# Forget bias and causal mask in a two-layer attention trunk: from matmul and mask passes to one fused vector operation with a prepared bias tile

## The reference, cut to what matters

```python
def forgetting_attention(q, k, v, log_f):
    scale = d ** -0.5
    c = jnp.cumsum(log_f, axis=-1)
    ...
        sc = (jnp.einsum('bhqd,bhkd->bhqk', qb, k, ...) * scale
              + (cq[..., :, None] - c[..., None, :]))
        sc = jnp.where(kpos[None, :] <= tq[:, None], sc, -jnp.inf)
        p = jax.nn.softmax(sc, axis=-1)
        return jnp.einsum('bhqk,bhkd->bhqd', p.astype(v.dtype), v)
```

## Time and profile before

| what | value |
|---|---|
| median of 3 runs | 568.36 us (568.06 to 568.9) |
| profiled execution | 567.49 us |
| its span, first to last instruction | 565.7 us |
| granted TensorE clock, mean | 1.000 |
| PE busy | 558.7 us (99% of the span) |
| DVE busy | 342.6 us (61%) |
| POOL busy | 268.2 us (47%) |
| ACT busy | 249.7 us (44%) |
| DMA | 47.82 MB, mean 85 GB/s |

### The profile page before, as it was taken

The page is one execution under the profiler, slowest core; times in us unless marked ns, Lnnn a source line. Parts: engine busy times, 40 slices in busy tenths (PEclk is TensorE's granted clock), DMA queues, the critical chain, the costliest instruction groups (busy, mean ns, idle before and its releaser), DMA issues.

```text
span 565.7 us, 9786 instructions
## 1 busy us (share of the span) xinstructions
PE 558.7 (99%) x3118; PEld 516.2 (91%) x3118; DVE 342.6 (61%) x824; ACT 249.7 (44%) x762; POOL 268.2 (47%) x320
## 2 busy tenths in 40 slices
PE   6999999999999999999999999999999999999998
PEld 4999999999999999888888999999999999998887
DVE  3788585859594949473553755656565646464621
ACT  5737272626263636152544635444444444442400
POOL 5857272727171818162656454545353536360700
PEclk9999999999999999999999999999999999999999
DMA  9823132313131313123423261415140615030221
GB/s 263 231 61 110 57 93 57 94 56 93 56 93 56 96 52 104 45 76 110 123 68 83 83 102 34 104 35 130 28 121 24 112 30 130 24 124 2 74 94 56
DMA packets 77068, 47.82 MB, mean 85 GB/s; under 512 B 3953, under 2 KB 71281, under 8 KB 77042
## 3 DMA queue, kind: packets, MB, share of 16 engines
q1 hardware_dynamic: 77040, 47.49, 31.5%
q10 hardware_dynamic: 2, 0.00, 0.0%
HBM read 45.39 MB, written 2.10 MB: 84 GB/s over the span
## 4 chain that ended last, share of the span: by engine, by line
PE 98%; DMA 1%; SPq 0%; DVE 0%; ACT 0%; issue 0%
PE banks L325 26%; PE banks L326 26%; PE banks L327 26%; PE banks L456 5%; PE banks L441 3%; PE banks L408 2%; PE banks L426 2%; PE banks L430 2%; PE banks L425 2%; PE banks L357 1%; DMA first_raw<-in_a_w_in_dram 1%; PE banks L429 1%; PE banks L482 0%; PE banks L483 0%; SPq L292 0%; DVE hT_lo L782 0%
## 5 line engine op out<-in xcount | busy, mean ns | idle before, releaser
L1061 POOL TENSOR_TENSOR w_lo<-w_raw,w_hi 128x512 fp32r<-128x512 f32 x147 | 188.3, 1311 | 63.0 <-ACT w_hi L586 63.0
L325 PE MATMUL banks<-w_hi,hT_hi 128*128 128x384 f32 x512 | 175.6, 343 | 1.0 <-DVE hT_lo L782 1.0
L327 PE MATMUL banks<-w_hi,hT_lo 128*128 128x384 f32 x512 | 171.6, 335 | 0.0
L326 PE MATMUL banks<-w_lo,hT_hi 128*128 128x384 f32 x512 | 171.6, 335 | 0.0
L1077 POOL TENSOR_TENSOR msq<-ssq,eps 128x2 f32<-128x2 f32 x64 | 14.3, 224 | 186.4 <-ACT junk L622 186.3
L325 PEld LDWEIGHTS banks<-w_hi,hT_hi 128*128 128x128 f32 x512 | 96.5, 188 | 1.9 <-POOL w_lo L1061 1.6
L326 PEld LDWEIGHTS banks<-w_lo,hT_hi 128*128 128x128 f32 x512 | 96.5, 189 | 0.1
L327 PEld LDWEIGHTS banks<-w_hi,hT_lo 128*128 128x128 f32 x512 | 96.3, 188 | 0.0
L586 ACT ACTIVATE w_hi<-w_raw 128x512 fp32r<-128x512 f32 x148 | 85.0, 646 | 20.2 <-DMA w_raw<-in_b_w_in_dram 14.4
L622 ACT ACTIVATE junk<-banks 128x128 bf16<-128x128 f32 x128 | 34.3, 274 | 115.8 <-PE banks L327 115.8
L906 DVE RECIPROCAL gz<-gz 128x128 f32<-128x128 f32 x64 | 58.1, 931 | 0.5
(11 more groups left out here) (113 smaller groups left out, 883.9 us busy)
## 6 DMA issues: line engine op xcount, KB each, us to landing
w_raw<-in_b_w_in_dram SPq DMA_DIRECT2D x64, 256.0 KB, 3.7
w_raw<-in_a_w_in_dram SPq DMA_DIRECT2D x52, 256.0 KB, 3.0
w_raw<-in_w_out_dram SPq DMA_DIRECT2D x32, 256.0 KB, 2.9
first_raw<-in_a_w_in_dram SPq DMA_DIRECT2D x12, 256.0 KB, 5.6
out_dram<-xs SPq DMA_DIRECT2D x7, 256.0 KB, 2.1
xs<-in_x_dram SPq DMA_DIRECT2D x3, 512.0 KB, 5.8
xs<-in_x_dram SPq DMA_DIRECT2D x2, 256.0 KB, 3.2
gz<-in_norm_g_dram SPq DMA_DIRECT2D x1, 512.0 KB, 3.7
```

Source lines behind the costliest of these rows:

```text
L325: pe.matmul(dst, ah, bh, start=first and m == 0, stop=False)
L326: pe.matmul(dst, ah, bl, start=False, stop=False)
L327: mm = pe.matmul(dst, al, bh, start=False, stop=last and m == n - 1)
L1061: pool.tensor_tensor(w_lo[:, slot, k, :], raw, f32(w_hi[:, slot, k, :]), ALU.subtract).then_inc(wlo_set, by)
```

## The change

- The bias matmul L429, `pick`, `crows`, `onehot` and their preparation (`set_pick`, `split_c`, the copy L709) go. Each score tile of layer 1 has 3 matmuls, as in layer 0.
- `maxima` becomes one `tensor_tensor_reduce` for a tile: it reads the scores in PSUM and a bias tile in SBUF, writes -(score + bias) to `probs` and the minimum of it to `negmax`. Three 1-element memsets of `gate` carry the waits for the scores. In layer 0 the bias tile is a constant `strip` (zeros, and the triangular mask in its last 128 columns). `exps` then works in place on `probs`, in SBUF, with scale -1.
- In layer 1 the bias tiles stand in SBUF, all 128 partitions alike. After `cumulate` SP writes the 8 cumulated rows to DRAM (`c_rows`), waits for that, and loads the row of head 0 into four tiles with DMAs that spread it over the partitions (`load_bias`; 256, 192, 128 and 64 KB). The rows of heads 1 to 7 are loaded in the same way in the middle of a later weight job, behind its chunk 4 and behind a wait for the maxima of the head before.
- POOL adds the triangle to the diagonal blocks of the four bias tiles (`mask_bias`) as the first thing in period(h) of layer 1.

```diff
-                if layer == 1:
-                    pe.wait_ge(c_set, 1)
-                    pe.wait_ge(pick_set, h + 1)
...
-                    if layer == 1:
-
-                        pe.matmul(dst, pick[:, s, :], crows[:, 0:w], start=False, stop=False)
```

```diff
             def load_job(layer, h, src_of, bias=False):
...
                     load_chunk(w_raw[:, k % RAW, :], src_of(k), raw_in[k % RAW])
+                    if bias and k == RAW:
+                        load_bias(h - 1)
...
+            def load_bias(h):
+
+                wait(sp, max_set, TILES * (HEADS + h) if not isinstance(h, int) or h else 0)
+                for t in T_ORDER:
+                    row = c_rows[bass.ds(h, 1), 0:P * (t + 1)].rearrange("o n -> (o n)")
+                    sp.dma_start(bias_of[t], row.partition_broadcast(P)).then_inc(bias_in, 16)
+
             for layer in range(LAYERS):
-                with sp.Fori(0 if layer else 2, HEADS) as h:
-                    load_job(layer, h, head_src(layer, h))
+                if layer == 1:
+                    for h in range(2):
+                        load_job(layer, h, head_src(layer, h))
+                    sp.wait_ge(f_step, 4)
+                    sp.dma_start(c_rows, f_all).then_inc(c_stored, 16)
+                    sp.wait_ge(c_stored, 16)
+                    load_bias(0)
+                with sp.Fori(2, HEADS) as h:
+                    load_job(layer, h, head_src(layer, h), bias=layer == 1)
                 for c in range(OUT_CHUNKS):
-                    load_job(layer, HEADS + c, out_src(layer, c))
+                    load_job(layer, HEADS + c, out_src(layer, c), bias=layer == 1 and c == 0)
```

```diff
             def exps(layer, h):
                 g = HEADS * layer + h
-                wait(act, p_turned, 3 * g)
                 for n, t in enumerate(T_ORDER):
...
+                    part = probs[:, P_COL[t]:P_COL[t] + P * (t + 1)]
+                    act.wait_ge(max_set, TILES * g + n + 1)
+                    act.activation(part, part, ACT.Exp, bias=negmax[:, t:t + 1], scale=-1.0,
+                                   accum_out=rowsum[:, t:t + 1]).then_inc(exp_set, 1)
```

```diff
             def maxima(layer, h):
...
                 wait(dve, exp_set, TILES * g)
+                wait(dve, p_turned, 3 * g)
+                if layer == 1:
+                    dve.wait_ge(bias_set, h + 1)
                 for n, t in enumerate(T_ORDER):
                     bank, col = S_AT[t]
...
+                    w = P * (t + 1)
+                    if n < 3:
+                        dve.wait_ge(s_done, 3 * g + n + 1)
+                        dve.memset(gate[0:1, n:n + 1], 0.0)
+                    dve.tensor_tensor_reduce(out=probs[:, P_COL[t]:P_COL[t] + w], in0=banks[:, bank, col:col + w],
+                                             in1=bias_of[t] if layer else strip[:, SEQ - w:], scale=-1.0,
+                                             scalar=NO_MIN, op0=ALU.add, op1=ALU.min,
+                                             accum_out=negmax[:, t:t + 1]).then_inc(max_set, 1)
```

```diff
+            def mask_bias(h):
+
+                pool.wait_ge(bias_in, 16 * TILES * (h + 1))
+                for t in T_ORDER:
+                    diag = bias_of[t][:, P * t:P * (t + 1)]
+                    added = pool.tensor_tensor(diag, diag, strip[:, SEQ - P:], ALU.add)
+                added.then_inc(bias_set, 1)
+
             def period(layer, h, s):
+                if layer == 1:
+                    mask_bias(h)
                 rstd_qk(layer, h + 1, 0)
...
             def last(layer):
+                if layer == 1:
+                    mask_bias(HEADS - 1)
                 split_w(layer, HEADS + 1, 1, range(KC))
```

More of the change, by code:

```diff
@@ L27 @@
 MASKED = -3.0e38
+NO_MIN = 3.0e38
 LO_ROW = 32
@@ L85, in build_trunk @@
         sin_t = sb("sin_t", [P, TILES, 2, P])
-        crows = sb("crows", [P, SEQ], F32R)
-        pick = sb("pick", [P, 2, P], F32R)
         ident = sb("ident", [P, P])
-        mask = sb("mask", [P, P])
+        one = sb("one", [1, P])
+        strip = sb("strip", [P, SEQ])
         junk = sb("junk", [P, 2, P], BF16)
-        onehot = sb("onehot", [P, HEADS])
         wf = sb("wf", [P, KC, LO_ROW + HEADS], F32R)
@@ L211, in build_trunk @@
                       (QT_BANK, t, slice(cols.start + CH // 2, cols.stop))]
-        spare = sin_t[:, :, :, :].rearrange("p a b n -> p (a b n)")
-        f_lo, f_all = spare[0:HEADS, 0:SEQ], spare[0:HEADS, SEQ:2 * SEQ]
-        f_exp = rot[:, :, :, :].rearrange("p a b n -> p (a b n)")[0:HEADS, :]
-        ones = cos_t[:, :, :, :].rearrange("p a b n -> p (a b n)")[0:HEADS, SEQ:2 * SEQ]
+        sin_flat = sin_t[:, :, :, :].rearrange("p a b n -> p (a b n)")
+        cos_flat = cos_t[:, :, :, :].rearrange("p a b n -> p (a b n)")
+        f_lo, f_exp, ones = sin_flat[0:HEADS, 0:SEQ], sin_flat[0:HEADS, SEQ:], cos_flat[0:HEADS, SEQ:]
+        f_all = rot[:, :, :, :].rearrange("p a b n -> p (a b n)")[0:HEADS, :]
+        bias_of = {3: sin_flat[:, 0:4 * P], 2: sin_flat[:, 4 * P:7 * P], 1: cos_flat[:, 2 * P:4 * P], 0: sin_flat[:, 7 * P:]}
+        c_rows = nc.dram_tensor("c_rows", (HEADS, SEQ), F32, kind="Internal").ap()
         def normed(layer, t):
@@ L240, in _, with load_job @@
             w_in = (a_w_in, b_w_in)
-            def load_job(layer, h, src_of):
+            def load_job(layer, h, src_of, bias=False):
                 j = JOBS * layer + h
@@ L340, in spread_gain @@
                 for half in range(2):
-                    pe.matmul(banks[:, GAIN_BANKS[half], :], f32(pick[0:1, 0, :]), gz[0:1, half, :],
+                    pe.matmul(banks[:, GAIN_BANKS[half], :], one[:, :], gz[0:1, half, :],
                               start=True, stop=True).then_inc(gain_spread, 1)
@@ L634, in exps @@
                 g = HEADS * layer + h
-                wait(act, p_turned, 3 * g)
                 for n, t in enumerate(T_ORDER):
-                    bank, col = S_AT[t]
-                    w = P * (t + 1)
-                    act.wait_ge(max_set, TILES * g + (n + 1 if n < 2 else TILES))
-                    act.activation(probs[:, P_COL[t]:P_COL[t] + w], banks[:, bank, col:col + w], ACT.Exp,
-                                   bias=negmax[:, t:t + 1], accum_out=rowsum[:, t:t + 1]).then_inc(exp_set, 1)
+                    part = probs[:, P_COL[t]:P_COL[t] + P * (t + 1)]
+                    act.wait_ge(max_set, TILES * g + n + 1)
+                    act.activation(part, part, ACT.Exp, bias=negmax[:, t:t + 1], scale=-1.0,
+                                   accum_out=rowsum[:, t:t + 1]).then_inc(exp_set, 1)
             def split_probs(layer, h):
@@ L705, in first @@
                 split_w(layer, 1, 1, (6, 7))
-                if layer == 1:
-                    act.wait_ge(f_step, 4)
-                    act.wait_ge(consts_set, 1)
-                    act.activation(crows[0:HEADS, :], f_all, ACT.Copy).then_inc(chi_set, 1)
                 exp_z(layer, 0)
@@ L910, in silu_part @@
                     dve.tensor_tensor(gz[:, 1, :], banks[:, Z_BANK, :], gz[:, 0, :], ALU.mult).then_inc(gate_set, 1)
-            def set_pick(h, s):
-                wait(dve, s_done, 3 * (HEADS + h - 1))
-                dve.tensor_scalar(pick[:, s, :], ident[:, :], 0.0, onehot[:, bass.ds(h, 1)],
-                                  ALU.mult, ALU.add).then_inc(pick_set, 1)
             def add_unit(layer, u):
@@ L946, in cumulate @@
                 dve.tensor_tensor_scan(f_all, ones, f_lo, 0.0, ALU.mult, ALU.subtract).then_inc(f_step, 1)
-            def split_c():
-                dve.wait_ge(chi_set, 1)
-                dve.tensor_tensor(crows[LO_ROW:LO_ROW + HEADS, :], f_all, f32(crows[0:HEADS, :]),
-                                  ALU.subtract).then_inc(c_set, 1)
             def first(layer):
@@ L998, in first @@
                     cumulate()
-                    dve.wait_ge(consts_set, 1)
-                    set_pick(0, 0)
-                    split_c()
                 split_qk(layer, 0)
@@ L1022, in period @@
                 low_y(layer, h)
-                if layer == 1:
-                    set_pick(h + 1, 1 - s)
                 split_qk(layer, h + 1)
@@ L1079, in rstd_qk @@
                 pool.tensor_tensor(rstd[:, t % 2, :], msq[:, t % 2, :], power[:, :], ALU.pow).then_inc(rstd_set, 1)
-            pool.memset(f32(pick[0:1, 0, :]), 1.0).then_inc(ones_row, 1)
+            pool.memset(one[:, :], 1.0).then_inc(ones_row, 1)
             pool.memset(ident[:, :], 0.0)
-            pool.memset(mask[:, :], 0.0)
-            pool.memset(onehot[:, :], 0.0)
-            pool.memset(f32(crows[:, :]), 0.0)
+            pool.memset(strip[:, :], 0.0)
             pool.memset(f32(wf[:, :, :]), 0.0)
```

31 lines of the change are left out of this document (8 added, 23 removed).

## The result

| | before | after |
|---|---|---|
| median of 5 runs | 568.36 us (567.86 to 569.48) | 571.99 us (571.53 to 573.46) |
| ratio | | 1.0064, 95 % interval 1.0045 to 1.0082 |
| profiled execution, its span | 567.49 us, 565.7 us | 573.46 us, 571.6 us |
| granted TensorE clock, mean | 1.000 | 0.997 |

The account below looks back on a forecast made before the run. The prediction took PE, busy 99% of the span, as the bound. Matmuls removed -5.1, head 0's stall +2.4 and later weights +0.3 gave -2.4 us: from 568.36 to 566.0 us, range 563.1 to 568.8.

Parts of the forecast that it names:

- Removed from PE: Four bias matmuls per head of layer 1 go: 0.64 us a head, 5.1 us for eight heads.
- Vector work: Fused masking and maxima in every head: 2.2 us (2.0 to 2.8 plus memsets) against 2.39 before, covered by 2.3 us of slack.
- POOL's masks: Four 128x128 additions before each period of layer 1: 1.9 us, costing nothing in heads 1 to 7.
- Spread of head 0: Four loads of 640 KB after the store in layer 1: bias in 4.55 us after first issue, at 319.6.
- the twin: Loads of 512 + 64 + 64 KB in the old trace, in 4.55 us after first issue, used to price head 0's spread.
- ACT's branch: Head 0, layer 1: ACT copies chunks 0 to 3 of head 2 before the exps; PE stalls 2.4 us.
- Weights of the heads 1 to 6: Bias loads delay chunks 5 to 7 past 24 us: 0 to 1.8 us stall per slow period, 0.3 us added for all.
- The weight queue becomes the bound: Rival: SP's queue at head 0 stalls PE 6.3 us, slow later heads add more; 571.1 us, chance 0.14.
- the covered case: Rival: head 0's stall nearly covered, chunks 1.0 us apart, stall 0 to 1.2 us; 563.9 us, chance 0.25.
- POOL's branch: Head 0, layer 1: bias in, four masks, then rstd, norm, maxima, exps, normalise; 0.7 us stall if alone.
- The dear operation: Rival: the fused operation costs more than 4.7 us a head; at 5 us, 568.4 us; chance 0.05.
- the matmuls free nothing: Rival: PE meets another wait of the same length in each period; 568.4 us, chance 0.03.

Follow-up runs that it names:

- the floor: The changed kernel without store, spreading loads and POOL's masks, layer 1 reading the constant strip: 563.04 us, ratio 0.9911.
- the two floors: The changed kernel without store, loads and masks, 563.04 us; and the kernel before without its bias matmul L429, 563.3 us.
- another source row: The changed kernel with all spreads read from a row of the norm gains in place of `c_rows`: 573.19 us, one run.
- shifted columns: The changed kernel with weight jobs 2 to 7 of layer 1 reading the columns of the head before: 570.58 us, one run.
- loads added to before: The complete kernel before plus the store and four spreads for heads 1 to 7 behind chunk 4, into unread tiles: 571.76 us, ratio 1.0068.

## Why the prediction failed, step by step

- **Removed from PE: right.** 5.1 us forecast; 5.0 by leaving out the matmul alone, 5.4 by the floor. The two gaps of the earlier trace rows overstate it a little: the gaps alternate between 27.94 and 27.96 in layer 0 and between 28.56 and 28.58 in layer 1, so the mean difference is 0.62 us and eight heads give 5.0.
- **Vector work: right.** Forecast 2.2 us for four fused operations, measured 1.7 from the first start to the work behind them (327.49 to 329.15); before it was 2.39. The operations take 686, 551, 419 and 285 ns by the groups of after (x8 in layer 1 | busy, mean ns) and overlap, as does the accumulator read of 83 ns. Exps from SBUF are 0.03 us longer each (724 ns for 512 columns, before 690). Both lie in the cover that I named.

```profile
L857 DVE CUSTOM_DVE_ANT_0 probs<-banks,sin_t 128x512 f32<-128x512 f32 x8 | 5.5, 686 | 0.0
...
L857 DVE CUSTOM_DVE_ANT_0 probs<-banks,sin_t 128x128 f32<-128x128 f32 x8 | 2.3, 285 | 0.0
```

- **POOL's masks: right.** 1.9 forecast, 1.7 measured, and free in the heads 1 to 7.
- **Store: right**, 1.5 us against 2.0.
- **Spread of head 0: the first term that failed.** 4.55 us forecast from the twin, 7.9 measured; "bias in" came 9.45 us after the scan and not 6.7. I matched the twin by bytes and took 3.7 us plus half a us of queue for the upper end, without asking what the source looks like. The twin's large piece was a row of 4 KB; these are rows of 2 KB and less. The Trainium skill's page "DMA: Bandwidth & Descriptors", which I weighed, would have given 2.0 us plus 640 KB at 436 GB/s, an estimate of 3.5 us. It states the figure for DMAs that GpSimd issues, and these are SP's; here 7.9 us were measured.
- **Which branch holds head 0: wrong.** I let ACT's branch decide (2.4 us) and gave POOL's 0.7. POOL's holds: its 0.7 plus the 2.75 us by which the bias came late (9.45 - 6.7) are 3.45, and the loss is 3.45, a miss of 1.05 us. In times, rstd is done at 326.92, plus 6.06 is 332.98, and PE turned at 333.04. That 6.06 I had called DVE's order (norm, maxima, exps, normalise); it is POOL's four subtractions, 5.03 us, and the 1.08 us of `normalise` behind them. Of ACT's branch the start was too early by the same late bias and the pace too slow: the fourth chunk came 4.1 us behind the bias (about 328.3 against 324.2), not 5.6. The two errors nearly cancel, so that the old ACT line would also end near 333; that is luck.
- **Weights of the heads 1 to 6: the term that decides.** The mechanism, the place (chunks 5 to 7 behind the spreads, period 2 first), the limit of 24 us into the period were right. The last chunk came 27.6 us in, 3.6 beyond the limit, and the stall is 3.24. My upper bound was 25.8, by bytes at the stretch's 113 GB/s (19.7 + 5.8 is 25.5, a slip of 0.3); the spreads took 12 us of the queue instead of 5.8. And within 0 to 1.8 us for each of three slow periods I put 0.3 in the sum for all: I chose near the lower end although the row nearest in time, the slow stretch itself, spoke for the upper. Measured: 3.24 + 0.75 us. In period 5 the last chunk landed 24.5 us in, which bears out the limit.
- **The clock: not in the forecast.** 1.6 us more behind the stall of period 2.
- **The balance.** -5.1 + 3.45 + 4.0 + 1.6 = +3.95 where I had -5.1 + 2.4 + 0.3 = -2.4. Of the 6.35 us between them the loads of the heads 1 to 6 are 3.7, the clock 1.6, head 0 1.05.
- **The rivals.** "The weight queue becomes the bound" gave 571.1 and a chance of 0.14: the right sign and nearly the right time, but the wrong place. It put 6.3 us at head 0 by slow chunks, and 1.5 in later heads. Head 0's chunks were fast, and it was the later heads that turned the result. In the covered case the condition came true (chunks 1.0 us apart, POOL's branch alone counts), but not its 0 to 1.2 us of stall, since it kept the 4.55 us spread. The dear operation and "the matmuls free nothing" are refuted by the two floors.
- **What I said would show it.** PE idle ahead of `turn_probs`, put down to `normalise`, and ACT idle for a chunk of head 2: both there, and yet ACT's branch was not the one. The chunk's pace, 1.0 us and not near 1.4, was a sign of being wrong that I had named, and it showed, as did the bias, in 9.45 us behind the scan and not 6.7. But a second wait, before `qkv` tile 2, was the larger, and I had passed over it: norm of tile 1 "had 1 to 2 us to spare" was checked, norm of tile 0, which frees the bank that PE writes next, was not.

## What to carry to other kernels

Price a transfer by a row with the same source pattern, above all where one row is spread over all partitions; here the same bytes were in 1.7 times as fast from 128 different rows. A load that isn't due soon belongs behind the last one that is: moving one line in the queue's order turned a loss of 0.6 % into a gain of 0.25 %. On an in-order engine, let a step that is ready (rstd) pass ahead of one that waits for a transfer (the masks), and count a long stall of PE as possibly more than its length.

## What the runs showed of the hardware

- One row of at most 2 KB, spread over 128 partitions: 640 KB took 7.9 us from first issue to last landing (12 us beside queued weights in the slow stretch). The same sizes from 128 different rows took 4.7 us; 512 KB from a row of 4 KB with two of 64 KB took 4.55.
- A stall of PE can be paid twice, when the clock falls behind it. After an idle time of 3.1 us PE ran at 1.2 GHz from about 406.1 to 409.5 and lost 1.6 us more; after 3.9 us, some 1.6 more. After 2.8 us (another source row) it ran 6.8 us at 1.2 GHz, and after 2.3 us (shifted columns) it fell as well, while after 2.4 us (loads added to before) and 2.2 us (another source row, period 2) the profiles show full clock. So the length of the idle time alone doesn't decide. Where only head 0's waits of 2.0 and 1.0 us were left, the profiled executions kept full clock, but the mean clock was 0.997 in 3 of 10 runs with head 0's bias alone and in 2 of 10 with the spreads behind chunk 7. The Trainium skill's "TensorE: Matmul & The Clock Gate" (section "Part 1: The HAM clock gate") says that the clock depends on how busy PE has been; the trace agrees, and adds that within a kernel that is 98 % busy one stall can be enough.
- `normalise`, a vector operation on SBUF, ended 1.06 to 1.08 us behind POOL's last chunk subtraction in each of the heads 0 to 6 of layer 1 (before, after, and the spreads behind chunk 7), whether it had started 0.6 or 1.2 us ahead of that end.
- A small store to DRAM with its wait took 1.5 us, less than any of the spreads behind it.
